# A hybrid encoder trunk on one core: attention maps turned by VectorE in blocks, heads turned by TensorE

## The chip, the cores and the metric

One core of one Trainium2 chip runs the whole program. The metric is the device time of one execution in microseconds (us); lower is better. TensorE does matrix products and transposes, VectorE, ScalarE and GpSimd do the elementwise work, and SyncE issues the transfers.

## The reference

Two requests of 256 tokens (512 columns together) pass two layers of width 1024. All is float32.

```python
for l in range(DEPTH):                                    # DEPTH = 2
    h = rmsnorm(x, g_mix[l])
    u_a, v_a, q, k, v_b, g_a, g_b = split(h @ w_in[l])    # each 1024 wide
    y_a = spatial_gating(u_a, v_a, ...)
    y_b = diff_attention(q, k, v_b, ...)                  # 8 heads, two maps each
    m = sigmoid(g_a) * (y_a @ w_br[l, 0]) + sigmoid(g_b) * (y_b @ w_br[l, 1])
    x = x + m @ w_out[l]
    x = x + conv_gated_mlp(rmsnorm(x, g_ffn[l]), ...)     # 2816 wide, conv of width 3
# diff_attention, for each head and block of 128 queries:
    logits = q @ k.T * scale + bias          # two maps of 256 keys
    p = softmax(logits)
    out = (p[0] - lam * p[1]) @ v            # 128 wide
    out = rmsnorm(out, sub_g) * (1 - lam_init)
```

## The kernel before

Each weight is cut into a high and a low float32r part, and each product of weights is three TensorE passes (high by high, high by low, low by high) of 128 rows and 512 columns. ScalarE writes the high part `w_hi` (lines 555 and 556), VectorE a small piece of the low part `w_lo` (line 986) and GpSimd the rest of it (line 494). A weight slot holds 256 columns of a matrix, and its two halves are two TensorE stretches of 24 passes each.

The attention of a layer has 32 units: a unit is one head, one request and one block of 128 queries, with both of its maps. The order of all engines is written out by hand. The outer loop `r` goes over four pairs of heads, the inner one `i` over the eight units of a pair; the unit's number in the layer is `a = 8 * r + i`. The text calls one step `(r, i)` a window. In a window TensorE runs one half of a slot of the input projection for the next pair (`feature_half` or `token_half`; in the last pair the columns of `u_a`), and behind it `values(a - 2)`, the product of a turned map with the values, then `turn`, which transposes the map of the unit before, and then `logits` of the unit two further on. So the projection is the bulk of the window, and attention's small products stand behind it.

VectorE's window begins, where `i` is even, with the low part of a weight (`split`). It goes on with `softmax_out(i)` (reciprocal, ratio of the two maps and their difference, `attn`), in some windows `head_scale` (which frees the `HEAD` bank for the next head's values) or `head_lo`, then `softmax_in(i + 1)` (bias and maximum). After that come pieces of the head's transpose (`head_move`: VectorE's transpose turns blocks of 32 by 32, so a head of 128 by 512 needs 16 instructions), the low parts of q and k (`qk_lo`) and the evacuation of the projection (`evac_round`, which waits for the window's TensorE half). ScalarE has, in order: the squares of a head and its norm, `w_hi`, the high parts of q and k, the copy of the turned map out of the `TRANS` bank (`turned`, line 654), and the exponentials of the next unit. The queues are in order on each engine, so what stands behind a waiting instruction waits too.

Waits that matter in TensorE's window: `values` needs the turned map (`attn_t_ok`) and, for the first unit of a head (`i` of 2 and 6, since `values` runs two windows late), `head_o_ok` from `head_scale`; the projection needs its weights and a free bank. Slots have two buffers, as have logits, maps and turned maps.

Of the kernel before, what the change touches and what calls it, by code (L numbers as in the profile page):

```python
# [108 lines left out]
def encoder_kernel(nc, x_prompt, x_sample, rel_bias, g_mix, w_in, sgu_g, sgu_w, sgu_b, lam_qk, sub_g,  # L109
# [47 lines left out]
    head_f = sb("head_f", 119, [P, HEADS - 1, N])  # L157
# [17 lines left out]
    head_sq = sb("head_sq", 191, [P, N])  # L175
# [77 lines left out]
    trans_done, attn_t_ok, pv_done = sem("trans_done"), sem("attn_t_ok"), sem("pv_done")  # L253
    head_sq_ok, head_ln_ok, head_rms_ok = sem("head_sq_ok"), sem("head_ln_ok"), sem("head_rms_ok")
    head_wt_ok, head_o_ok, head_t = sem("head_wt_ok"), sem("head_o_ok"), sem("head_t")
    head_moved = sem("head_moved")
# [60 lines left out]

    def moved_n(l, h):

        return l * 4 * (HEADS - 1) + 4 * (h + 1)  # L320
# [218 lines left out]
    def _(sc):  # L539
# [65 lines left out]
        for l in range(DEPTH):  # L605
# [42 lines left out]
            def turned(r, i):  # L648

                a, j, (_h, _r, qt) = 8 * r + i, i // 2, units(i)  # L650
                sc.wait_ge(trans_done, l * UNITS + a + 1)
                if a >= 4:
                    sc.wait_ge(pv_done, l * UNITS + a - 3)
                nc.scalar.activation(attn_t[j % 2][:, :, qt * P:(qt + 1) * P],
                                     bank[TRANS][:, 0:2 * P].rearrange("p (k q) -> p k q", k=2), ACT.Copy)\
                  .then_inc(attn_t_ok, 1)

            def head_square(a):
                h, t = a // 4, a % 4
                sc.wait_ge(pv_done, l * UNITS + a + 1)  # L660
                if a:
                    sc.wait_ge(head_sq_ok, l * UNITS + a)
                nc.scalar.activation(head_sq[:, t * P:(t + 1) * P], bank[HEAD][:, t * P:(t + 1) * P], ACT.Square,
                                     scale=map_inv[:, h % 2, t, 0:1], accum_out=head_ssq[:, t:t + 1]).then_inc(head_sq_ok, 1)
# [10 lines left out]
            def head_hi(h):  # L675
                if h < HEADS - 1:
                    sc.wait_ge(head_moved, moved_n(l, h))
                    turned_head = head_f[:, h, :]
                else:
                    sc.wait_ge(head_t, l + 1)  # L680
                    turned_head = bank[TRANS][:, :]
                nc.scalar.activation(yb_hi[:, h, :], turned_head, ACT.Copy, scale=par[:, C_SUBS:C_SUBS + 1])\
                  .then_inc(yb_hi_ok, 1)
# [54 lines left out]
            for r in range(PAIRS):  # L738
                for i in range(8):
# [9 lines left out]
                    attention_window(r, i)  # L749
                    if r + 1 < PAIRS and i in (4, 5):  # L750
# [27 lines left out]
            turned(PAIRS - 1, 6)  # L778
            head_square(UNITS - 2)
            turned(PAIRS - 1, 7)  # L780
# [116 lines left out]
    def _(ve):  # L897
# [77 lines left out]
        for l in range(DEPTH):  # L975
# [24 lines left out]
            def evac_round(p, place_n, half):  # L1000
# [16 lines left out]
                if n == 3:  # L1017
                    if p == 0 and half == 0:
                        ve.wait_ge(rms_col_ok, l + 1)
                    if p == 2 and half == 0:  # L1020
                        ve.wait_ge(spilled, l * 16 + 16)
                    if p == 3 and half == 0:
                        ve.wait_ge(pv_done, l * UNITS + 16)
# [21 lines left out]
            def softmax_out(r, i):  # L1045
# [9 lines left out]
                if a >= 2:  # L1055
                    ve.wait_ge(trans_done, l * UNITS + a - 1)
                nc.vector.scalar_tensor_tensor(attn[i % 2][:, :], logit[i % 2][:, 1, :], map_ratio[i % 2][:, :],
                                               logit[i % 2][:, 0, :], ALU.mult, ALU.add).then_inc(attn_ok, 1)

            def head_scale(h):  # L1060
# [4 lines left out]
                if h:  # L1065
                    ve.wait_ge(head_moved, moved_n(l, h - 1))
# [4 lines left out]
            def head_move(h, c):  # L1071

                if c == 0:
                    ve.wait_ge(head_o_ok, l * HEADS + h + 1)
                    if h == HEADS - 2:
                        ve.wait_ge(qk_done, l * UNITS + UNITS)
                for a in range(4):
                    src = head_o[32 * a:32 * a + 32, :].rearrange("q (t c d) -> q t c d", t=4, c=4)[:, :, c, :]
                    dst = head_f[32 * c:32 * c + 32, h, :].rearrange("d (t a q) -> d t a q", t=4, a=4)[:, :, a, :]
                    last = nc.vector.transpose(dst, src)  # L1080
                last.then_inc(head_moved, 1)

            def head_lo(h):
                ve.wait_ge(yb_hi_ok, l * HEADS + h + 1)
                turned_head = head_f[:, h, :] if h < HEADS - 1 else bank[TRANS][:, :]
                nc.vector.scalar_tensor_tensor(yb_lo[:, h, :], turned_head, par[:, C_SUBS:C_SUBS + 1],
# [20 lines left out]
            for r in range(PAIRS):  # L1107
                if r == 0:
                    softmax_in(0, 0)
                for i in range(8):  # L1110
                    if i % 2 == 0:
                        split(4 * (r + 1) + i // 2 + 1)
                    softmax_out(r, i)
# [4 lines left out]
                    if r and i == 3:  # L1118
                        head_lo(2 * r - 2)
                    if r and i == 7:  # L1120
# [11 lines left out]
                    if r + 1 == PAIRS and i == 7:  # L1132
                        for c in range(2):
                            head_move(HEADS - 2, c)
# [614 lines left out]
```

## Time and profile before

| what | before |
|---|---|
| median of 3 runs | 1709.09 us (1708.75 to 1709.99) |
| the profiled execution | 1709.8 us, its span 1708.0 us |
| busy share of TensorE, VectorE, ScalarE, GpSimd | 100%, 55%, 44%, 39% |
| granted TensorE clock, mean | 0.999 |

The span is what the profiler records from the first to the last instruction; the time of the execution lies 1.8 us above it. Busy shares are means over the whole span; the attention stages lie at 57 to 267 us and 900 to 1110 us.

### The profile page before, as it was taken

How to read it: one execution, taken by the hardware profiler on the slowest of the kernel's cores; microseconds unless marked ns; L12 is line 12 of the kernel's file. 1: busy time of each engine (PE TensorE's matmuls, PEld its weight loads, DVE VectorE, ACT ScalarE, POOL GpSimd, SP SyncE). 2: the span in 40 equal slices, each digit the busy share in tenths (PEclk: the TensorE clock that was granted, in tenths of full speed). 3: DMA queues.
4: the chain of work that ended last, by engine and by line, in shares of the span. 5: the costliest groups of instructions: out<-in, count | busy, mean ns of one | idle time of the engine just before them, and what ended most of it. 6: DMA issues, size and time to landing. Idle time of an engine off the chain costs nothing.

```text
span 1708.0 us, 22288 instructions
## 1 busy us (share of the span) xinstructions
PE 1699.7 (100%) x7907; PEld 1419.2 (83%) x7907; DVE 945.8 (55%) x1544; ACT 747.7 (44%) x1352; POOL 662.8 (39%) x806
## 2 busy tenths in 40 slices
PE   9999999999999999999999999999999999999998
PEld 7888888888888888888888888888888888888886
DVE  4678876433337766631146888755433476666112
ACT  4676654222345444432256666432223444444222
POOL 3444333333344444434344344333333444444222
PEclk9999999999999999999999999999999999999999
DMA  7422222323232222222353222322242232322222
GB/s 248 135 75 74 87 86 99 99 79 143 98 99 98 98 98 96 92 95 92 108 182 99 75 74 75 124 75 98 74 147 99 96 101 98 98 98 98 87 92 80
DMA packets 146150, 173.93 MB, mean 102 GB/s; under 512 B 2928, under 2 KB 129570, under 8 KB 145570
## 3 DMA queue, kind: packets, MB, share of 16 engines
q1 hardware_dynamic: 145954, 172.96, 30.5%
q8 instruction: 39, 0.64, 0.2%
q14 instruction: 29, 0.24, 0.0%
q10 hardware_dynamic: 128, 0.09, 0.0%
HBM read 166.73 MB, written 6.31 MB: 101 GB/s over the span
## 4 chain that ended last, share of the span: by engine, by line
PE 99%; DVE 0%; ACT 0%; issue 0%; POOL 0%; POOLq 0%; ACTq 0%
PE bank L1448 25%; PE bank L1447 25%; PE bank L1449 25%; PE bank L1482 3%; PE bank L1483 3%; PE bank L1484 3%; PE bank L1719 2%; PE bank L1717 2%; PE bank L1718 2%; PE bank L1505 2%; PE bank L1532 2%; PE bank L1607 1%; PE bank L1516 1%; PE bank L1384 1%; PE bank L1428 1%; PE bank L1637 0%
## 5 line engine op out<-in xcount | busy, mean ns | idle before, releaser
L494 POOL TENSOR_TENSOR w_lo<-raw,w_hi 128x256 fp32r<-128x256 f32 x776 | 627.6, 841 | 1010.0 <-ACT w_hi L556 1010.0
L1447 PE MATMUL bank<-xg_hi,w_hi 128*128 128x512 f32 x1344 | 525.9, 391 | 0.0
L1448 PE MATMUL bank<-xg_lo,w_hi 128*128 128x512 f32 x1344 | 523.4, 389 | 0.0
L1449 PE MATMUL bank<-xg_hi,w_lo 128*128 128x512 f32 x1344 | 523.1, 389 | 0.0
L1449 PEld LDWEIGHTS bank<-xg_hi,w_lo 128*128 128x128 f32 x1344 | 252.3, 188 | 52.7
L1447 PEld LDWEIGHTS bank<-xg_hi,w_hi 128*128 128x128 f32 x1344 | 252.5, 188 | 52.3 <-issue 1.0
L1448 PEld LDWEIGHTS bank<-xg_lo,w_hi 128*128 128x128 f32 x1344 | 252.5, 188 | 51.7 <-issue 1.0
L986 DVE TENSOR_TENSOR w_lo<-raw,w_hi 128x768 fp32r<-128x768 f32 (+2 forms) x146 | 124.9, 856 | 209.9 <-ACT w_hi L555 209.7
L556 ACT ACTIVATE w_hi<-raw 128x1280 fp32r<-128x1280 f32 (+2 forms) x147 | 194.0, 1319 | 0.0
L555 ACT ACTIVATE w_hi<-raw 128x768 fp32r<-128x768 f32 (+2 forms) x147 | 110.4, 751 | 175.1 <-PE bank L1449 90.5
L816 ACT ACTIVATE conv<-up,conv_par 128x512 f32<-128x512 f32 x88 | 71.8, 816 | 129.2 <-DVE up L1248 129.2
L1248 DVE TENSOR_TENSOR up<-bank,rms 128x512 f32<-128x512 f32 x88 | 60.7, 690 | 99.8 <-PE bank L1449 80.6
L1254 DVE SCALAR_TENSOR_TENSOR conv<-up,conv_par,conv 128x510 f32<-128x510 f32 x88 | 77.9, 885 | 47.3 <-ACT conv L816 47.1
L644 ACT ACTIVATE logit<-logit,neg_max 128x256 f32<-128x256 f32 x128 | 64.1, 502 | 89.6 <-DVE neg_max L1042 89.2
L1482 PE MATMUL bank<-w_hi,xg_hi 128*128 128x512 f32 x224 | 87.6, 391 | 0.0
L1483 PE MATMUL bank<-w_hi,xg_lo 128*128 128x512 f32 x224 | 87.5, 390 | 0.0
L1484 PE MATMUL bank<-w_lo,xg_hi 128*128 128x512 f32 x224 | 87.2, 389 | 0.0
L1257 DVE SCALAR_TENSOR_TENSOR conv<-up,conv_par,conv 128x510 f32<-128x510 f32 x88 | 73.8, 839 | 3.1
L1080 DVE STREAM_TRANSPOSE head_f<-head_o 32x128 f32<-32x128 f32 x224 | 67.7, 302 | 3.6
L768 ACT ACTIVATE gate<-gate 128x512 f32<-128x512 f32 x32 | 20.0, 631 | 111.7 <-DVE gate L1207 57.9
L1717 PE MATMUL bank<-w_hi,g_hi 128*128 128x512 f32 x176 | 68.7, 390 | 0.0
L1719 PE MATMUL bank<-w_lo,g_hi 128*128 128x512 f32 x176 | 68.5, 389 | 0.0
(187 smaller groups left out, 2580.1 us busy)
## 6 DMA issues: line engine op xcount, KB each, us to landing
raw<-in_w_in SPq DMA_DIRECT2D x55, 1024.0 KB, 5.1
raw<-in_w_up SPq DMA_DIRECT2D x44, 1024.0 KB, 5.0
raw<-in_w_br SPq DMA_DIRECT2D x16, 1024.0 KB, 5.0
raw<-in_w_down SPq DMA_DIRECT2D x12, 1024.0 KB, 5.0
raw<-in_w_out SPq DMA_DIRECT2D x8, 1024.0 KB, 4.9
raw<-in_w_down SPq DMA_DIRECT2D x8, 896.0 KB, 4.6
x_spill<-x_res SPq DMA_DIRECT2D x2, 2048.0 KB, 7.5
x_res<-x_spill SPq DMA_DIRECT2D x2, 2048.0 KB, 9.5
```

What stands on the lines that cost most here:

```text
L494: last = nc.gpsimd.tensor_tensor(w_lo[p_][:, k, :], raw[p_][:, k, :], f32(w_hi[p_][:, k, :]), ALU.subtract)
L555: nc.scalar.activation(w_hi[s % 2][:, 0:kd(s), :], raw[s % 2][:, 0:kd(s), :], ACT.Copy).then_inc(hi_split, 1)
L556: nc.scalar.activation(w_hi[s % 2][:, kd(s):n, :], raw[s % 2][:, kd(s):n, :], ACT.Copy).then_inc(hi_split, 1)
L986: nc.vector.tensor_tensor(w_lo[p_][:, 0:kd(s), :], raw[p_][:, 0:kd(s), :], f32(w_hi[p_][:, 0:kd(s), :]), ALU.subtract).then_inc(lo_vector, 1)
L1447: nc.tensor.matmul(out, w_hi[w][:, k, cols], x_hi[:, a, :], start=first and k == 0, stop=False)
L1448: nc.tensor.matmul(out, w_hi[w][:, k, cols], x_lo[:, a, :], start=False, stop=False)
L1449: mm = nc.tensor.matmul(out, w_lo[w][:, k, cols], x_hi[:, a, :], start=False, stop=last and k == kt - 1)
L1482: nc.tensor.matmul(bank[t][:, :], xg_hi[:, a, cols], wide_hi[:, k, :], start=first, stop=False)
L1483: nc.tensor.matmul(bank[t][:, :], xg_lo[:, a, cols], wide_hi[:, k, :], start=False, stop=False)
L1484: mm = nc.tensor.matmul(bank[t][:, :], xg_hi[:, a, cols], wide_lo[:, k, :], start=False, stop=last)
L1717: nc.tensor.matmul(out[:, :], g_hi[:, k0 + k, cols], wide_hi[:, k, :], start=c + k == 0, stop=False)
L1719: mm = nc.tensor.matmul(out[:, :], g_hi[:, k0 + k, cols], wide_lo[:, k, :], start=False, stop=last)
```

## The change

The map of a unit is no longer transposed by TensorE. VectorE keeps the maps of two units in one tile (`attn[pair % 2]`, 128 by 2 by 256) and turns both in blocks of 32 by 32 straight into `attn_t` (`turn_maps`). This takes 16 instructions for two units, in two parts of eight: part 0 after `softmax_in` of the odd window, part 1 at the head of the next even window, ahead of its `softmax_out`. Seven of eight heads of a layer, which VectorE turned before, are turned by TensorE as the eighth was (`turn_head`, four transposes, behind `logits` in the windows of `i` 7 and 3), and `head_hi` and `head_lo` read them out of the `TRANS` bank. ScalarE no longer copies turned maps, and evacuates the projected values (two instructions of 128 by 512 in each of the windows 6 and 7) for pairs 1 to 3 with `values_out`; VectorE keeps those of pair 0.

```diff
-    attn = [sb(f"attn{i}", 183 + i, [P, SEQ]) for i in range(2)]
+    attn = [sb(f"attn{i}", kb, [P, 2, SEQ]) for i, kb in enumerate((183, 191))]
...
-            def turned(r, i):
...
+            def values_out(p, half):
+                sc.wait_ge(proj_done, proj_n(l, S_R + 4 * p + 3, half))
+                if p == 2 and half == 0:
+                    sc.wait_ge(spilled, l * 16 + 16)
+                if p == 3 and half == 0:
+                    sc.wait_ge(pv_done, l * UNITS + 16)
+                for t in (2 * half, 2 * half + 1):
+                    dst = va[:, p - 1:p + 1, t, :] if p % 2 else v_tok[p // 2][:, :, t, :]
+                    nc.scalar.activation(dst, bank[t][:, :].rearrange("p (two c) -> p two c", two=2), ACT.Copy,
+                                         scale=rms_col[:, t:t + 1]).then_inc(evacuated, 1)
...
             def attention_window(r, i):
-                if r and i == 2:
+                if r and i == 0:
                     head_hi(2 * r - 2)
-                if r and i == 6:
+                if r and i == 4:
                     head_hi(2 * r - 1)
-                if r and i < 2:
-                    turned(r - 1, 6 + i)
-                if i >= 2:
-                    turned(r, i - 2)
...
                     attention_window(r, i)
+                    if r + 1 < PAIRS and i >= 6:
+                        values_out(r + 1, i - 6)
...
-                if a >= 2:
-                    ve.wait_ge(trans_done, l * UNITS + a - 1)
-                nc.vector.scalar_tensor_tensor(attn[i % 2][:, :], logit[i % 2][:, 1, :], map_ratio[i % 2][:, :],
+                nc.vector.scalar_tensor_tensor(attn[(i // 2) % 2][:, i % 2, :], logit[i % 2][:, 1, :], map_ratio[i % 2][:, :],
...
-            def head_move(h, c):
...
+            def turn_maps(pair, part):
+                if part == 0:
+                    ve.wait_ge(attn_ok, l * UNITS + 2 * pair + 2)
+                    if pair >= 2:
+                        ve.wait_ge(pv_done, l * UNITS + 2 * pair - 2)
+                for c in (2 * part, 2 * part + 1):
+                    for a in range(4):
+                        src = attn[pair % 2][32 * a:32 * a + 32, :, :].rearrange("q u (t c k) -> q u t c k", t=2, c=4)[:, :, :, c, :]
+                        dst = attn_t[pair % 2][32 * c:32 * c + 32, :, :].rearrange("k t (u a q) -> k u t a q", u=2, a=4)[:, :, :, a, :]
+                        last = nc.vector.transpose(dst, src)
+                last.then_inc(attn_t_ok, 1)
...
                     if i % 2 == 0:
                         split(4 * (r + 1) + i // 2 + 1)
+                    if i % 2 == 0 and r + i:
+                        turn_maps(4 * r + i // 2 - 1, 1)
                     softmax_out(r, i)
...
-                    if r and 2 <= i <= 5:
-                        head_move(2 * r - 1, i - 2)
-                    if r and i < 2:
-                        head_move(2 * r - 2, 2 + i)
-                    if r + 1 < PAIRS and i >= 6:
-                        head_move(2 * r, i - 6)
...
+                    if i % 2:
+                        turn_maps(4 * r + i // 2, 0)
...
             def values(a):
-                pe.wait_ge(attn_t_ok, l * UNITS + a + 1)
+                pe.wait_ge(attn_t_ok, l * UNITS + 2 * (a // 2) + 2)
...
                     if a >= 2:
                         values(a - 2)
-                    if a:
-                        turn((a - 1) // 8, (a - 1) % 8)
                     if i + 2 < 8:
                         logits(r, i + 2)
                     elif r + 1 < PAIRS:
                         logits(r + 1, i - 6)
+                    if i == 3 and r:
+                        turn_head(2 * r - 1)
+                    if i == 7:
+                        turn_head(2 * r)
```

## Rows read from the trace of the kernel before

**Rows 1.** The page, busy us (share of the span) and instructions of each engine.
```profile
PE 1699.7 (100%) x7907; PEld 1419.2 (83%) x7907; DVE 945.8 (55%) x1544; ACT 747.7 (44%) x1352; POOL 662.8 (39%) x806
```

**Rows 2.** The page, chain that ended last, by engine.
```profile
PE 99%; DVE 0%; ACT 0%; issue 0%; POOL 0%; POOLq 0%; ACTq 0%
```

**Rows 3.** Windows by head pair, layer 0: length, PE, PEld, DVE, ACT, POOL busy, clock.
```profile
57.56:109.10 51.54, 51.54 (x261) 43.84 (x260) 37.81 (x73) 34.47 (x87) 23.16 (x29) 1.00 0.31 102
109.10:162.00 52.90, 52.90 (x274) 45.21 (x273) 44.48 (x98) 36.52 (x96) 20.75 (x28) 1.00 0.25 80
...
214.82:267.20 52.38, 52.38 (x269) 44.71 (x268) 38.36 (x90) 26.59 (x82) 18.42 (x26) 1.00 0.30 101
```

**Rows 4.** TensorE in order of time, around one window: start, us, engine, line.
```profile
201.61 0.60 PE L1532 MATMUL bank<-v_tok,attn_t 128*128 128x128 f32 x4
202.05 0.38 PE L1516 MATMUL bank<-ident,attn 128*128 128x128 f32 x2
202.19 0.36 PE L1505 MATMUL bank<-k_hi,q_st 128*128 128x256 f32 x1
...
202.75 0.40 PE L1482 MATMUL bank<-w_hi,xg_hi 128*128 128x512 f32 x1
...
208.22 0.61 PE L1532 MATMUL bank<-v_tok,attn_t 128*128 128x128 f32 x4
```

**Rows 5.** TensorE's weight loads in order of time, the same window.
```profile
201.94 0.25 PEld L1516 LDWEIGHTS bank<-ident,attn 128*128 128x128 f32 x2
202.16 0.19 PEld L1505 LDWEIGHTS bank<-k_hi,q_st 128*128 128x128 f32 x1
```

**Rows 6.** The chain in order of time: eight transposes of the gating weights.
```profile
40.50 0.87 PE bank L1574 x8
```

**Rows 7.** VectorE's groups in 109.1 to 162 us: busy, mean ns, idle before, releasers.
```profile
L1080 DVE STREAM_TRANSPOSE head_f<-head_o 32x128 f32<-32x128 f32 x32 | 9.7, 302 | 0.5
...
L996 DVE TENSOR_TENSOR q_st<-qk_f,q_st 64x512 fp32r<-64x512 f32 x4 | 3.6, 909 | 0.1
L1016 DVE TENSOR_TENSOR qk_f<-bank,rms 128x512 f32<-128x512 f32 x4 | 2.8, 691 | 2.3 <-PE bank L1449 2.2
...
L986 DVE TENSOR_TENSOR w_lo<-raw,w_hi 128x256 fp32r<-128x256 f32 x4 | 1.7, 419 | 3.6 <-ACT w_hi L555 3.6
...
L1026 DVE TENSOR_SCALAR v_tok<-bank,rms_col 128x512 f32<-128x512 f32 x2 | 1.4, 747 | 0.0
L1026 DVE TENSOR_SCALAR va<-bank,rms_col 128x512 f32<-128x512 f32 x2 | 1.4, 747 | 1.7 <-PE bank L1484 1.7
```

**Rows 8.** VectorE in order of time: window (2, 6), then (3, 6), then eight transposes.
```profile
203.94 0.42 DVE L986 TENSOR_TENSOR w_lo<-raw,w_hi 128x256 fp32r<-128x256 f32 x1 [2.53 <-ACT w_hi L555]
204.28 0.16 DVE L1050 RECIPROCAL map_inv<-exp_sum 128x2 f32<-128x2 f32 x1
...
205.13 0.16 DVE L1063 TENSOR_TENSOR map_inv<-map_inv,head_rms 128x4 f32<-128x4 f32 x1
...
205.93 0.68 DVE L1038 SCALAR_TENSOR_TENSOR logit<-bank,bias_t 128x512 f32<-128x512 f32 x1
...
207.25 1.24 DVE L1080 STREAM_TRANSPOSE head_f<-head_o 32x128 f32<-32x128 f32 x4
...
256.90 0.96 DVE L986 TENSOR_TENSOR w_lo<-raw,w_hi 128x768 fp32r<-128x768 f32 x1 [1.55 <-ACT w_hi L555]
...
260.39 0.68 DVE L1038 SCALAR_TENSOR_TENSOR logit<-bank,bias_t 128x512 f32<-128x512 f32 x1
...
264.48 2.52 DVE L1080 STREAM_TRANSPOSE head_f<-head_o 32x128 f32<-32x128 f32 x8
```

**Rows 9.** ScalarE in order of time, before the same window.
```profile
203.50 0.40 ACT L555 ACTIVATE w_hi<-raw 128x256 fp32r<-128x256 f32 x1
```

**Rows 10.** ScalarE's groups over the span: busy, mean ns, idle before.
```profile
L691 ACT ACTIVATE junk<-va 128x256 f32<-128x256 f32 x32 | 13.2, 412 | 0.9
...
L682 ACT ACTIVATE yb_hi<-bank,par 128x512 fp32r<-128x512 f32 x2 | 1.4, 690 | 3.2 <-PE bank L1540 3.2
```

More of the change, by code:

```diff
@@ L675, in head_hi @@
             def head_hi(h):
[L676 to L682, printed above, removed]
+                sc.wait_ge(head_t, l * HEADS + h + 1)
+                nc.scalar.activation(yb_hi[:, h, :], bank[TRANS][:, :], ACT.Copy, scale=par[:, C_SUBS:C_SUBS + 1])\
                   .then_inc(yb_hi_ok, 1)
@@ L1017, in evac_round @@
                 if n == 3:
-                    if p == 0 and half == 0:
+                    if half == 0:
                         ve.wait_ge(rms_col_ok, l + 1)
[L1020 to L1023, printed above, removed]
                     for t in (2 * half, 2 * half + 1):
@@ L1069, in head_scale @@
                                         inv.to_broadcast([P, 4, P]), ALU.mult).then_inc(head_o_ok, 1)
-            def head_move(h, c):
[L1073 to L1081, printed above, removed]
+            def turn_maps(pair, part):
[9 more added lines that the diff above has]
+                last.then_inc(attn_t_ok, 1)
             def head_lo(h):
                 ve.wait_ge(yb_hi_ok, l * HEADS + h + 1)
-                turned_head = head_f[:, h, :] if h < HEADS - 1 else bank[TRANS][:, :]
-                nc.vector.scalar_tensor_tensor(yb_lo[:, h, :], turned_head, par[:, C_SUBS:C_SUBS + 1],
+                nc.vector.scalar_tensor_tensor(yb_lo[:, h, :], bank[TRANS][:, :], par[:, C_SUBS:C_SUBS + 1],
                                                f32(yb_hi[:, h, :]), ALU.mult, ALU.subtract).then_inc(yb_lo_ok, 1)
@@ L1117, in _ @@
                         head_scale(2 * r - 1)
-                    if r and i == 3:
+                    if r and i == 0:
                         head_lo(2 * r - 2)
-                    if r and i == 7:
+                    if r and i == 4:
                         head_lo(2 * r - 1)
@@ L1139, in _ @@
                             qk_lo(r + 1, i - 1)
-                        evac_round(r + 1, i // 2, i % 2)
+                        if r and i == 0:
+                            ve.wait_ge(evacuated, evac_n(l, slot_evac(S_R + 4 * r + 3, 1)))
+                        if i < 4:
+                            evac_round(r + 1, i // 2, i % 2)
                     else:
                         s, half = S_U + i // 2, i % 2
+                        if i == 0:
+                            ve.wait_ge(evacuated, evac_n(l, slot_evac(S_U - 1, 1)))
                         ve.wait_ge(proj_done, proj_n(l, s, half))
@@ L1148, in _ @@
                         nc.vector.tensor_reduce(va_rms[:, :], va_sq[:, :, :], AX.X, ALU.add).then_inc(va_sum_ok, 1)
-            for c in range(2, 4):
-                head_move(HEADS - 2, c)
+            turn_maps(UNITS // 2 - 1, 1)
             head_lo(HEADS - 2)
@@ L1508, in logits @@
                 mm.then_inc(qk_done, 1)
-            def turn(r, i):
-                a = 8 * r + i
-                pe.wait_ge(attn_ok, l * UNITS + a + 1)
-                if a:
-                    pe.wait_ge(attn_t_ok, l * UNITS + a)
-                for kt in range(2):
-                    mm = nc.tensor.transpose(bank[TRANS][:, kt * P:(kt + 1) * P], attn[i % 2][:, kt * P:(kt + 1) * P],
-                                             ident[:, :])
-                mm.then_inc(trans_done, 1)
             def values(a):
@@ L1535, in values, with turn_head @@
                 mm.then_inc(pv_done, 1)
-            def turn_last_head():
-                pe.wait_ge(head_o_ok, l * HEADS + HEADS)
+            def turn_head(h):
+                pe.wait_ge(head_o_ok, l * HEADS + h + 1)
+                if h:
+                    pe.wait_ge(yb_lo_ok, l * HEADS + h)
                 for t in range(4):
@@ L1629, in _ @@
                         else:
-                            turn_last_head()
+                            turn_head(HEADS - 1)
                         bank_free(s, half)
```

26 lines of the change are left out of this document (4 added, 22 removed).

## The prediction

> **What bounds the kernel now.** I read the page's busy table and the chain first, then the attention windows by stretch, then each engine's order of time inside one window. TensorE is busy for 1699.7 of 1708.0 us, and the chain is 99% TensorE [rows 1, 2]; the granted clock is full in every attention stretch [rows 3]. So a TensorE instruction taken away shortens the span at once, and work on VectorE costs nothing only while VectorE is ready before TensorE asks. VectorE's 55% is a mean: for the second head pair it is busy 44.48 of 52.90 us, 84%, before anything is added [rows 3]. Inside a window (call V the moment at which TensorE reaches `values`), the period is 208.22 - 201.61 = 6.61 us, of which 208.22 - 202.75 = 5.47 us are the projection and 1.14 us the small products [rows 4].
>
> **TensorE: removed and added.** By starts of matmuls a pair of map transposes takes 202.19 - 202.05 = 0.14 us [rows 4]; by starts of weight loads, which is what these short instructions queue for, 202.16 - 201.94 = 0.22 us [rows 5]. Eight transposes in a row take 0.87 us, 0.11 each [rows 6], which speaks for 0.22; the lower bound is 0.14. 64 units save 64 x 0.22 = 14.1 us (9.0 at the bound). Fourteen heads come back with four transposes each: 56 x 0.11 = 6.1 us. Net -7.9 us, and -2.9 at the bound. A window then takes 6.39 us, the windows 3 and 7 with a head's transposes 6.83; a full pair of heads 52.9 - 8 x 0.22 + 2 x 0.44 = 52.0 us.
>
> **VectorE: the sum.** Its transposes follow each other at 2.52 / 8 = 0.315 us [rows 8]. Before, each of 14 heads takes 16: 224 instructions, 70.6 us. After, each of 32 pairs of units takes 16: 512 instructions, 161.3 us. The tile they write has one more level of stride than before; the page has no such instruction, so from below I take the 302 ns of the plain form [rows 7], which is hardly less, and from above a third more, the ratio of 909 to 691 ns between two elementwise passes over 512 columns [rows 7]: 0.40 us. I take 0.315, since each row is the same 32 by 128 elements. Away from VectorE go 24 evacuations of projected values at 0.75 us [rows 7], 18 us; `head_lo` only changes its source. 161.3 - 70.6 - 18 makes +73 us on VectorE, nearly all of it inside 420 us of attention.
>
> Per head pair: in the second stretch VectorE's true waits are 2.2, 1.7 and 3.6 us, 7.5 together [rows 7], so its order of work takes 52.9 - 7.5 = 45.4 us. It loses 32 transposes (10.1) and four evacuations (3.0) and gains 64 transposes (20.2): 52.5 us, against 52.0 for TensorE. With no wait at all it no longer fits. The first pair comes to 50.8 against 50.4 us (37.8 busy and 0.8 of gaps, less 8 transposes and four evacuations, and 56 transposes more), the last to 49.3 against 51.1 (38.4 and 0.8, 32 less and 64 more) [rows 3].
>
> The Trainium skill (VectorE: DVE Perf Modes, "The three transpose paths") gives 390 ns for TensorE and 311 ns for VectorE on 128 by 128 in bf16, and its "Rules for kernel authors" send a 128 by 128 transpose to TensorE where PSUM will do. By that figure VectorE's 128 map blocks would cost 128 x 0.311 = 40 us, an estimate from that page, and it would have 81 us to spare against the change's sum. The trace has 302 ns for an instruction that covers only 32 partitions [rows 7], so four of them for a block, and its rows decide.
>
> **What then waits.** The turned map and `head_scale` now stand behind eight transposes (8 x 0.315 = 2.53 us) at the head of each even window, and TensorE's `values`, and all behind it, waits for them. Window (2, 6) shows the timing: V of window 5 is 201.61; ScalarE writes `w_hi` from 203.50, VectorE starts `split` at 203.94, V + 2.33 [rows 4, 8, 9]. `softmax_out` runs from 204.28 to 205.13 (0.85) and `head_scale` to 205.93 (0.80) [rows 8]. With part 1 between, `head_o_ok` comes at V + 2.33 + 0.34 + 2.53 + 0.85 + 0.80 = V + 6.85; TensorE's next V is at V + 6.39. That is a stall of 0.45 us where there was none, even if VectorE is never late. In window (3, 6) the low part is larger: from 256.90 to 260.39 are 3.49 us, now 6.02 [rows 8]; V of window 5 is there 201.61 + 8 x 6.61 = 254.46, so `head_o_ok` comes at V + 2.44 + 6.02 = V + 8.46, a stall of 2.1 us.
>
> VectorE's windows, summed from these terms (split 0.34, part 2.53, `softmax_out` 0.85 to 1.3 beside GpSimd, `softmax_in` 1.4 from 205.93 on, `qk_lo` 1.4 to 2.0 around two times the 0.91 us of its row, evacuation 0.61, `head_lo` 0.66): i 0 to 7 take 6.5, 6.9, 8.5, 6.8, 7.9, 4.8, 5.9 and 4.9 us. TensorE's 6.39 or 6.83 lies below that from 1 to 4, so lag piles up there. Walking the second pair from V of the last window of the first pair as zero:
> ScalarE now has `values_out` behind it (two at 0.69, the row of a PSUM read of that size, 0.61 apart [rows 10]) and in every other pair four squares of `va` with their reads, 0.5 apiece, before `w_hi`: VectorE begins window 0 at 4.2 (2.1 in the third pair) instead of 1.4. `values` of window 0 comes at 7.1 (stall 0.3). Window 1 ends on VectorE at 17.6, V of 1 is 13.5. In window 2 `head_o_ok` is at 17.6 + 4.5 = 22.1, TensorE at 19.9: stall 2.2. Window 4: the turned map at 35.8, TensorE at 35.3: 0.5. Window 6: VectorE begins at 45.6, `head_o_ok` at 50.2, TensorE at 48.6: 1.6. The pair ends at 56.6, against 52.9 before: +3.7 us. The third pair by the same walk, with its earlier start, stalls 0.4, 0.5 and 1.5: +1.5. The fourth stalls 0.3, 0.8 and 2.1, less what it saves: +1.9. The first starts without a lead, since in layer 0 its second window already runs late (part 0 puts VectorE's window 2 at V - 0.3): stalls of 2.6, 1.3 and 0.9, +3.5; in layer 1 0.5, 1.2 and 0.9, +1.3. Layer 0: 10.6, layer 1: 8.4, together +19 us with TensorE's saving already in it.
>
> ScalarE loses 64 copies and gets 24 evacuations, a little less in all; it has 16 us free in each stretch [rows 3], so it costs only through the order told above. GpSimd's low parts have some 3 us to spare after `w_hi`, so they hide. The weight transfers hang on GpSimd and are issued that much later, also hidden.
>
> From the profiled execution: 1709.8 + 19 = 1728.8 us; it lies 0.7 above the median, so 1728 for the runs shown.
>
> **Rivals.**
> *VectorE keeps up, TensorE's instructions decide.* Then only the 72 fewer transposes count: 1709.1 - 7.9 = 1701 us (1706 at the bound), faster. For it: TensorE bounds now, and waits of VectorE are 8 us in a pair of heads. Against it: the sum of 52.5 in 52.0, and the 6.85 against 6.39. It decides if VectorE's extra 2.53 us in windows 2 and 6 shrinks below about 2.1. Chance 0.11.
> *Only the order hurts.* VectorE is never behind, the stalls are the fixed ones: 0.45 in window 6 of three pairs, 2.1 in the last, 0.1 in three windows 2, some 3.8 us a layer. 7.6 - 7.9: 1709 us, no change. It holds if VectorE's idle time is enough to soak up the lag, against the sum. Chance 0.09.
> *VectorE saturated, as walked.* 1728 us. Chance 0.68.
> *The new output pattern is slow.* At 0.40 us, 512 x 0.085 = 43 us more, of which seven eighths lie where VectorE already paces: 1728 + 37 = 1765 us. Against it: element counts are the same, only the strides differ. Chance 0.07.
> *The stalls slow the clock.* A gap here is at most 2.6 us, and the records show full clock in all stretches [rows 3]; a fall in the granted clock to half within a stall would double the 0.23 us passes behind it. Nothing in the trace bears it out: 0.05, at around 1745 us.
>
> **The numbers.** A change within 0.2% (3.4 us) can't be told from none. Slower: the last three, 0.80; same: 0.09; faster: 0.11. The range leaves out the fast rival and the slow pattern: from 1709, the fixed stalls alone, to 1746; the likeliest case by itself, with 1 us either way in each pair of heads and VectorE's terms within 2%, 1718 to 1740.
>
> **What would show it.** The chain of waits would name VectorE's transposes and `head_scale` ahead of TensorE's `values` products, 15 to 40 times with 0.3 to 2.6 us each, some 27 us in sum; the stretches would be 53 to 57 us, VectorE above 90% busy in the first three; transposes on VectorE at 302 ns and 512 in number; TensorE's `values` followed at once by `logits`, 0.22 us sooner. It is wrong if the stretches come out near 52 us with no idle time on TensorE, if the transposes have another duration, or if the wait is on ScalarE's evacuation of values.

## The result, and the profile after

The changed kernel takes 1777.49 us (median of 5 runs, 1776.53 to 1779.67) against 1709.09 (1708.75 to 1709.99): ratio 1.0401, 95% interval 1.039 to 1.0412. That is 68 us slower, where 19 was predicted. The profiled execution has a span of 1774.7 us against 1708.0, so 66.7 us are to be found in the trace. From the page of the changed kernel: busy us of each engine; the chain of work that ended last, followed back from the last instruction, by engine; and two groups of instructions (busy, mean ns of one, idle before, releaser).

```profile
PE 1717.9 (97%) x7835; PEld 1426.5 (80%) x7835; DVE 1029.1 (58%) x1808; ACT 741.4 (42%) x1312; POOL 659.1 (37%) x806
...
PE 79%; DVE 15%; ACT 3%; issue 3%; POOL 0%; ACTq 0%; POOLq 0%
...
L1061 DVE STREAM_TRANSPOSE attn_t<-attn 32x128 f32<-32x128 f32 x512 | 154.7, 302 | 7.2
...
L1501 PE MATMUL bank<-v_tok,attn_t 128*128 128x128 f32 x256 | 43.6, 296 | 48.8 <-DVE head_o L1047 42.0
```

Two things differ from [rows 1, 2]. TensorE was idle for 8.3 us in all and is now for 56.8, of which 48.8 stand in front of the `values` products: 21 waits, 14 of them for `head_o` (42.0 us) and the other seven for `attn_t` (6.8 us). And TensorE's busy time went *up* by 18.2 us with 72 instructions fewer. Instructions that got fewer and yet busier are running slower, and the windows say so. Stretches of the attention part of layer 0: length, PE, PEld, DVE, ACT, POOL busy, the granted clock, DMA share, GB/s.

```profile
57.00:110.00 53.00, 46.86 (x217) 38.99 (x216) 45.70 (x105) 28.62 (x64) 21.53 (x29) 0.94 0.24 80
110.00:167.00 57.00, 52.27 (x254) 44.03 (x255) 48.06 (x116) 37.39 (x98) 15.72 (x22) 0.94 0.23 74
167.00:222.00 55.00, 49.52 (x235) 41.25 (x234) 48.03 (x113) 28.39 (x69) 20.48 (x28) 0.94 0.20 67
222.00:280.00 58.00, 51.30 (x242) 42.65 (x241) 45.27 (x115) 28.25 (x81) 18.50 (x26) 0.94 0.20 65
```

The clock of 1.00 of [rows 3] is 0.94 in each. TensorE in order of time around the first wait shows where it falls (start, us of one, idle before in brackets):

```profile
79.02 1.22 PE L1501 MATMUL bank<-v_tok,attn_t 128*128 128x128 f32 x4 [3.55 <-DVE attn_t L1061]
79.89 0.56 PE L1484 MATMUL bank<-k_hi,q_st 128*128 128x256 f32 x1
...
81.32 0.63 PE L1427 MATMUL bank<-xg_lo,w_hi 128*128 128x512 f32 x1
81.74 0.63 PE L1428 MATMUL bank<-xg_hi,w_lo 128*128 128x512 f32 x1
...
84.66 0.40 PE L1426 MATMUL bank<-xg_hi,w_hi 128*128 128x512 f32 x1
84.90 0.40 PE L1427 MATMUL bank<-xg_lo,w_hi 128*128 128x512 f32 x1
...
88.09 0.60 PE L1501 MATMUL bank<-v_tok,attn_t 128*128 128x128 f32 x4
88.45 0.36 PE L1484 MATMUL bank<-k_hi,q_st 128*128 128x256 f32 x1
...
94.47 0.60 PE L1501 MATMUL bank<-v_tok,attn_t 128*128 128x128 f32 x4
```

```profile
76.00:80.00 4.00, 0.98 (x5) 0.98 (x5) 3.77 (x13) 0.84 (x2) 3.04 (x5) 0.72 0.00 0
80.00:84.00 4.00, 4.00 (x14) 3.32 (x13) 3.82 (x8) 2.01 (x7) 0.00 (x0) 0.50 0.78 262
84.00:88.00 4.00, 4.00 (x18) 3.29 (x17) 3.84 (x11) 3.05 (x8) 0.00 (x0) 0.93 0.00 0
```

The second fence has the stretches of the same place, columns as above. After a wait of 3.55 us passes of 512 columns start 0.42 us apart (81.32 to 81.74) instead of 0.24 (84.66 to 84.90), at a granted clock of 0.50, the lower level, 1.2 GHz; from 84.66 on it is the full one. This window lasts 88.09 - 79.02 = 9.07 us, where the next, undisturbed one lasts 94.47 - 88.09 = 6.38. So this wait costs 3.55 us and then 2.7 us more. The other waits of layer 0, read in the same way, cost 1.6 to 1.7 us behind 1.83, 2.25, 2.84, 3.23 and 3.58 us of waiting and 2.3 behind 4.41; the wait of 2.62 us cost 0.1 behind it, and those of 0.29 us 0.1. Layer 1 has waits of the same length with another price: one of 2.25 us at 1049.27 us costs 1.7 behind it, at a granted clock of 0.67 to 0.79, and one of 2.25 us at 1110.46 costs 0.1, at a clock of 1.00; its wait of 1.83 us costs 0.1, where that of layer 0 cost 1.7. So the length of a wait doesn't fix its price. The Trainium skill (TensorE: Matmul & The Clock Gate, "Part 1: The HAM clock gate") has a clock that falls to half when the array has been idle; the trace agrees behind 12 of the 21 waits, all of 1.83 us or more, and shows no such price behind the other nine, the longest of 2.62 us (granted clock 1.00 in and behind it).

**The sum.** Waits +48.8 us; transposes -7.9 as worked out; that leaves 66.7 - 48.8 + 7.9 = 25.8 us that are neither. By the lengths of the windows, the slower stretches behind the 21 waits are 13.6 us in layer 0 and 10.2 in layer 1, and a window that ends in a wait is 0.16 us longer than its like (6.55 for 6.39), 3.4 us in all. That makes 27, so the sum closes within 1.4 us, and 23 of it stand behind the 12 waits with the lower clock.

### The profile page after: what moved, and what is told of

It reads as the page before. It is cut to its first block, busy times and chain, and to the rows that moved or that the text cites. A ratio compares the mean times of both kernels' runs of the same rounds, so it can differ in the third digit from the quotient of the medians.

```text
span 1774.7 us, 22236 instructions
## 1 busy us (share of the span) xinstructions
PE 1717.9 (97%) x7835; PEld 1426.5 (80%) x7835; DVE 1029.1 (58%) x1808; ACT 741.4 (42%) x1312; POOL 659.1 (37%) x806
## 4 chain that ended last, share of the span: by engine, by line
PE 79%; DVE 15%; ACT 3%; issue 3%; POOL 0%; ACTq 0%; POOLq 0%
PE bank L1426 21%; PE bank L1427 21%; PE bank L1428 21%; DVE attn_t L1061 5%; PE bank L1689 2%; PE bank L1690 2%; PE bank L1691 2%; DVE attn L1037 1%; DVE logit L1020 1%; PE bank L1463 1%; PE bank L1462 1%; DVE neg_max L1024 1%; PE bank L1461 1%; DVE map_ratio L1034 1%; DVE q_st L982 1%
## 5 line engine op out<-in xcount | busy, mean ns | idle before, releaser
L1426 PE MATMUL bank<-xg_hi,w_hi 128*128 128x512 f32 x1344 | 531.6, 396 | 0.0
L972 DVE TENSOR_TENSOR w_lo<-raw,w_hi 128x768 fp32r<-128x768 f32 (+2 forms) x146 | 126.6, 867 | 212.2 <-ACT w_hi L549 211.9
L1061 DVE STREAM_TRANSPOSE attn_t<-attn 32x128 f32<-32x128 f32 x512 | 154.7, 302 | 7.2
L1501 PE MATMUL bank<-v_tok,attn_t 128*128 128x128 f32 x256 | 43.6, 296 | 48.8 <-DVE head_o L1047 42.0
L1501 PEld LDWEIGHTS bank<-v_tok,attn_t 128*128 128x128 f32 x256 | 39.1, 202 | 60.6 <-issue 47.5
```

The costliest lines, as they stand in the source:

```text
L972: nc.vector.tensor_tensor(w_lo[p_][:, 0:kd(s), :], raw[p_][:, 0:kd(s), :], f32(w_hi[p_][:, 0:kd(s), :]), ALU.subtract).then_inc(lo_vector, 1)
L1426: nc.tensor.matmul(out, w_hi[w][:, k, cols], x_hi[:, a, :], start=first and k == 0, stop=False)
```

## Why head_o comes late: the moved work meets GpSimd

VectorE in order of time in window (0, 6), the case worked out ahead as V + 6.85, then GpSimd in the same window:

```profile
103.82 0.42 DVE L972 TENSOR_TENSOR w_lo<-raw,w_hi 128x256 fp32r<-128x256 f32 x1 [1.40 <-ACT w_hi L549]
104.28 2.53 DVE L1061 STREAM_TRANSPOSE attn_t<-attn 32x128 f32<-32x128 f32 x8
106.84 0.17 DVE L1032 RECIPROCAL map_inv<-exp_sum 128x2 f32<-128x2 f32 x1
107.04 0.57 DVE L1034 SCALAR_TENSOR_TENSOR map_ratio<-map_inv,par,exp_sum 128x1 f32<-128x1 f32 x1
107.65 0.91 DVE L1037 SCALAR_TENSOR_TENSOR attn<-logit,map_ratio 128x256 f32<-128x256 f32 x1
108.48 0.68 DVE L1043 TENSOR_TENSOR map_inv<-map_inv,head_rms 128x4 f32<-128x4 f32 x1
109.19 0.69 DVE L1047 TENSOR_TENSOR head_o<-bank,map_inv 128x512 f32<-128x512 f32 x1
109.80 0.68 DVE L1020 SCALAR_TENSOR_TENSOR logit<-bank,bias_t 128x512 f32<-128x512 f32 x1
```

```profile
105.46 5.05 POOL L488 TENSOR_TENSOR w_lo<-raw,w_hi 128x256 fp32r<-128x256 f32 x7 [9.19 <-ACT w_hi L550]
```

V is 100.86 here. The instruction behind `head_o` starts at 109.80, V + 8.94. Term by term against the 6.85: the split begins at V + 2.96 (2.33), the split takes 0.46 (0.34), the transposes 2.56 (2.53), `softmax_out` 1.64 (0.85), `head_scale` 1.32 (0.80). Before, `softmax_out` and `head_scale` ran directly behind the split and were nearly done when GpSimd's low part began; put back by 2.5 us, they lie in the middle of its 5.05 us. The product of a map of 256 columns takes 0.91 instead of 0.48 us (the first line below, from the kernel before) and the 4-column product of `head_scale` 0.68 instead of 0.16 [rows 8]. The two together take 2.96 us instead of 1.65. In C (the change, as it is called below) this happens to 12 of the 14 heads that TensorE waits for: their small product takes 0.68 us with GpSimd at work throughout, and the two steps together 2.63 to 2.98. The transposes (one input) and the two instructions that read PSUM (`head_o` 0.69, `logit` 0.68) keep their times.

```profile
204.73 0.48 DVE L1057 SCALAR_TENSOR_TENSOR attn<-logit,map_ratio 128x256 f32<-128x256 f32 x1
...
205.57 4.91 POOL L494 TENSOR_TENSOR w_lo<-raw,w_hi 128x256 fp32r<-128x256 f32 x7 [9.00 <-ACT w_hi L556]
```

The Trainium skill (SBUF — State Buffer, "SBUF: two separate sides") has a port pair that VectorE and GpSimd hold by an exclusive lock, on VectorE's side for instructions with two inputs in SBUF against a GpSimd instruction that reads SBUF. The instructions just listed agree with it. Over the traces of all versions the 4-column product takes 0.15 to 0.17 us wherever GpSimd's records leave it free, and 0.65 to 0.70 where they cover it, with five exceptions: in number 12 below it takes 0.15 twice (at 254.89 and 282.13 us) and 0.54 once, in number 11 twice 0.41. So GpSimd at work doesn't slow it in every place, which no run here explains.

The price stood in the trace of the kernel before, in the one window of each layer where `softmax_out` and `head_scale` already run beside GpSimd. It is window (3, 6), whose whole length the prediction used and whose parts it didn't look at:

```profile
258.23 0.91 DVE L1057 SCALAR_TENSOR_TENSOR attn<-logit,map_ratio 128x256 f32<-128x256 f32 x1
259.06 0.70 DVE L1063 TENSOR_TENSOR map_inv<-map_inv,head_rms 128x4 f32<-128x4 f32 x1
...
258.12 3.69 POOL L494 TENSOR_TENSOR w_lo<-raw,w_hi 128x256 fp32r<-128x256 f32 x5 [8.88 <-ACT w_hi L556]
```

## The experiments

Times are medians; each ratio is against the kernel before on the same chip. TensorE's waits are those listed in front of the `values` products. The change is named C, and a band is the range of times that an expectation gave.

**1. Part 1 of the turned map behind head_scale, in windows 2 and 6.**

```
 softmax_out(r, i); head_scale(...)
+if i % 4 == 2:
+    turn_maps(4 * r + i // 2 - 1, 1)      # was ahead of softmax_out
```

> Only the order on VectorE is changed: in windows 2 and 6 the second part of the map transposes stands behind head_scale, not ahead of softmax_out. Theory A (place and GpSimd: 14 of the 21 waits of values are for head_o, 42.0 of 48.8 us, because eight transposes stand ahead of softmax_out and head_scale and push both into GpSimd's low part, where they took 2.96 instead of 1.65 us): the two go back to about 1.7 us, values waits for the turned map instead, each wait is 1.2 us shorter, 17 us in all, and with shorter waits the half clock goes in part: 1745 to 1760 us. Theory B (VectorE is simply full, the order is nothing): within 5 us of 1777. Both: 512 transposes at 302 ns.

1759.53 us, ratio 1.0286 (1.0262 to 1.0311), its four runs from 1755.1 to 1763.5: 18 us of the 68 come back. `softmax_out` and `head_scale` are back at 1.77 us in eight of the 14 places and take 2.67 to 3.04 in the six that still have GpSimd beside them. The waits are 39.7 us, 39.5 of them for `attn_t`: windows 2 and 6 need both the turned map and `head_o`, so an exchange of the two mostly changes the name of what is late.

**2. All 16 transposes of a pair in the odd window.**

```
 if i % 2:
     turn_maps(4 * r + i // 2, 0)
+    turn_maps(4 * r + i // 2, 1)
```

> Both parts of the map transposes stand in the odd window, behind softmax_in, and none at the head of an even window. Theory A: head_scale comes 2.5 us sooner after VectorE's even window begins, window 5, which has room, takes the part that stood in window 6, so the waits before windows 6 nearly vanish and those before windows 2 shrink: 1725 to 1745 us, better than scale_first. Theory B (VectorE is full): the same 161 us of transposes are in the queue, 1765 to 1780 us.

1761.94 us, 1.031 (1.0292 to 1.0327), waits 41.7 us, again mostly for `head_o`. It fell between the two expectations, and by its runs (1759.6 to 1765.1) it can't be told from number 1. `softmax_out` and `head_scale` still take 2.86 to 3.08 us in all 14 places: with no transposes ahead of them in the window, VectorE is late enough that GpSimd's low part is under way when it gets there.

**3. TensorE kept busy in front of the head_o waits** (20 transposes of the identity ahead of each of the 14).

```
 if a % 4 == 0 and a:
+    for _ in range(20):
+        nc.tensor.transpose(bank[TRANS][:, 0:P], ident[:, :], ident[:, :])
     pe.wait_ge(head_o_ok, l * HEADS + a // 4)
```

> Twenty transposes of the identity (2.2 us) are added on TensorE ahead of each of the 14 waits for head_o (all of them into a part of a PSUM bank that is free), nothing else. The waits are 2.3 to 4.4 us long, so the added work lies inside them. Theory C (the half clock behind each wait, mean granted clock 0.983 over the span, is a cost of its own, up to 30 us): the granted clock comes back to 1.00 in the stretches behind the waits, and the time falls to 1750 to 1765 us although work was added. Rival (only the waits count, the clock falls into time that is lost anyway): 1775 to 1785 us.

1764.06 us, 1.0324 (1.0306 to 1.0341): 13.4 us *less* than C, with 280 matmuls added and `head_o` no earlier by design. The same wait as above at 109 us, and its stretches (columns as above):

```profile
106.04 2.40 PE L1500 MATMUL bank<-ident 128*128 128x128 f32 x20 [0.25 <-DVE attn_t L1061]
109.10 0.71 PE L1505 MATMUL bank<-v_tok,attn_t 128*128 128x128 f32 x4 [0.66 <-DVE head_o L1047]
```

```profile
57.00:112.00 55.00, 50.54 (x249) 42.13 (x249) 46.65 (x109) 30.33 (x70) 21.55 (x28) 0.97 0.25 80
112.00:167.00 55.00, 52.48 (x269) 43.49 (x267) 47.42 (x116) 36.13 (x94) 15.93 (x23) 1.00 0.22 74
167.00:222.00 55.00, 52.82 (x284) 44.74 (x285) 49.66 (x116) 30.21 (x75) 19.71 (x27) 1.00 0.24 77
```

The clock is 1.00 in the stretches behind the filled waits, and 0.97 in the one that holds the unfilled wait for `attn_t`. The windows behind the filled waits last 6.47 to 6.50 us (the last of each layer 5.9), near the 6.39 of an undisturbed one; in C 11 of the 14 last 7.6 to 8.9. This shows the slow clock as a cost of its own, apart from the idle time. Only 13.4 us come back and not 20, presumably because VectorE is late for a quicker TensorE too; that was not measured.

**4. Half of the map transposes left out** (256 of 512 transposes; TensorE's instructions as in C; the turned tiles are set to zero once in each layer).

```
-for c in (2 * part, 2 * part + 1):
+for c in (2 * part,):
```

> Half of the map transposes is left out (four instead of eight instructions in each part, 256 fewer, so half of the turned maps is zero and the values' products are incomplete); a clearing of the two tiles is added once in each layer (about 1 us on VectorE). All waits, their order and TensorE's instructions stay. If VectorE's time is all that costs, with about 42 of 52 us in a pair of heads it is ready in time: 1701 to 1706 us, TensorE's 7.9 us saving shown whole. If another part of the change costs (the values evacuated by ScalarE, the heads' transposes in the TRANS bank, a chain of waits), 1715 us or more.

1724.81 us, 1.0095 (1.0078 to 1.0112). VectorE has 81 us less to do, more than the 73 that the change adds, so by its sum it would keep up; the clock is full (0.999), and still TensorE waits 18.8 us. That is the second case of the expectation, 1715 us or more, by a cause that it didn't list: `softmax_out` and `head_scale` take 2.83 to 2.87 us in 12 of the 14 places (2.59 in the other two). So VectorE's sum is only part of the story. Its waits for `head_o` (releaser; us, times, longest):

```profile
PE bank L1505 <- DVE head_o L1047: 17.4, 14, 2.3
```

**5. The same with part 1 behind head_scale in windows 2 and 6** (edits 4 and 1 together).

> As half_turned (half of the map transposes left out, half of the turned maps zero), and the second part stands behind head_scale in windows 2 and 6. In half_turned 20 us of waits were left, nearly all for head_o, with VectorE far from full. Theory A (place and GpSimd): softmax_out and head_scale run before GpSimd's low part and take 1.65 instead of 2.83 us, head_o comes some 2.5 us sooner, no wait is left: 1700 to 1705 us. Theory B (something else, for instance ScalarE's later w_hi, delays VectorE's even windows): waits of 10 us and more stay, 1712 us or more.

1710.75 us, 1.0004 (0.9995 to 1.0014). All 14 waits for `head_o` are gone; 5.4 us in four waits for `attn_t` are left. The distance to number 4 is 14 us for a place in the order alone, and the two steps are at 1.77 us in 12 of the 14 places. The time is still above theory A's band of 1700 to 1705: the waits that are left, the longest of 3.01 us with 1.4 us behind it, were to be none. TensorE's window lasts 178.04 - 171.65 = 6.39 us in its trace, the figure worked out ahead:

```profile
171.65 0.60 PE L1507 MATMUL bank<-v_tok,attn_t 128*128 128x128 f32 x4
...
178.04 0.60 PE L1507 MATMUL bank<-v_tok,attn_t 128*128 128x128 f32 x4
```

**6. C with the values evacuated by VectorE again.**

```
-if r + 1 < PAIRS and i >= 6:
-    values_out(r + 1, i - 6)            # ScalarE
-if i < 4:
-    evac_round(r + 1, i // 2, i % 2)
+evac_round(r + 1, i // 2, i % 2)        # VectorE, all rounds
```

> The change with one part undone: the projected values of pairs 1 to 3 are evacuated by VectorE again. If VectorE's time sets the pace, 24 instructions of 0.75 us come back on a full engine: 1785 to 1800 us. Rival (ScalarE's evacuations delay w_hi and with it VectorE's window 0 by 2 to 4 us, which is a cost of the change): 1765 to 1777 us.

1765.44 us, 1.0321 (1.0304 to 1.0339): 12 us less than C, though the evacuations add 18 us of work to the engine that is late. TensorE's waits fall from 48.8 to 42.8 us. C's trace shows where: ScalarE at the end of the first head pair, then VectorE, behind it.

```profile
116.69 1.27 ACT L681 ACTIVATE va<-bank,rms_col 128x512 f32<-128x512 f32 x2 [0.93 <-PE bank L1463]
117.85 0.42 ACT L670 ACTIVATE junk<-va 128x256 f32<-128x256 f32 x1
...
120.29 0.41 ACT L549 ACTIVATE w_hi<-raw 128x256 fp32r<-128x256 f32 x1
```

```profile
120.73 0.42 DVE L972 TENSOR_TENSOR w_lo<-raw,w_hi 128x256 fp32r<-128x256 f32 x1 [3.69 <-ACT w_hi L549]
```

`w_hi` stands behind two evacuations and four squares of `va` on ScalarE, and VectorE is idle for 3.69 us until it comes. Over the whole span VectorE waits 211.9 us for `w_hi` in C and 188.3 here.

**7. The kernel before with that evacuation on ScalarE, and nothing else.**

> The kernel before with one part of the change alone: the projected values of pairs 1 to 3 are evacuated by ScalarE. TensorE's instructions are those of before and nobody waits: 1709 us, within 1 us. If ScalarE's evacuations delay w_hi past what TensorE can bear: 1712 us or more.

1708.8 us, 0.9997 (0.9988 to 1.0007). Alone it costs nothing, although VectorE waits for `w_hi` longer, 237.4 us over the span where the kernel before has 209.7: TensorE doesn't come to wait for it. So the same edit costs 0 or 12 us, by who waits behind VectorE in turn.

**8. Three of four pairs of units on VectorE, the third by TensorE and ScalarE**, with part 1 behind `head_scale` in window 2.

> A mixed version with the whole computation: of the four pairs of units in a pair of heads, VectorE turns three, and the third (units 4 and 5) goes through TensorE and the copy by ScalarE as before; in window 2 the second part stands behind head_scale. VectorE's order is some 47.5 us of 52. TensorE saves 48 x 0.22 = 10.6 us and gets 6.1 us of heads back: 1704.7 us if it never waits. Theory A: 1705 to 1710 us. Theory B (VectorE must be far below full before TensorE stops waiting, since the lag of windows 1 to 4 is what counts): 1715 to 1730 us.

1744.8 us, 1.0208 (1.0191 to 1.0225); waits 27.2 us, the large ones (2.1 to 5.1 us) all for `attn_t` at window 2. That is slower than both expectations had it: the relief stood at window 6, the crowd at window 2.

**9. The first of four pairs by TensorE and ScalarE instead**, both parts of the third in window 5.

```
+if i in (1, 2):
+    turn(r, i - 1)                       # TensorE; ScalarE copies it out
-if i % 2 == 0 and r + i:
+if i in (0, 4) and r + i:
     turn_maps(4 * r + i // 2 - 1, 1)
-if i % 2:
+if i % 2 and i > 1:
     turn_maps(4 * r + i // 2, 0)
+if i == 5:
+    turn_maps(4 * r + 2, 1)
```

> Another mixed version with the whole computation, three of four pairs of units turned by VectorE as in three_of_four, but the pair that TensorE and ScalarE turn is the first (units 0 and 1, whose parts stood in windows 1 and 2), and both parts of the third pair stand in window 5. No part of the transposes is left in windows 2 and 6. If the lag of windows 0 to 2 is what three_of_four lost 35 us to (its waits were for the turned map of pair 0, 12 of 14 us in layer 0), it goes: 1704 to 1710 us, with 0.3 to 0.5 us at window 0 of some head pairs left. If VectorE's total of some 47.5 of 52 us is too much in any order: 1720 us or more.

1729.65 us, 1.0121 (1.0106 to 1.0137), the second case of the expectation, though number 11 will show that its reason, too large a total in any order, is not the one: eight waits for `head_o` of 1.04 to 2.64 us are left, and seven small ones of at most 0.47.

**10. Number 9 with the values on VectorE**, as in number 6.

> As first_by_tensor, with the projected values of pairs 1 to 3 evacuated by VectorE again. In values_vector the same step back took 12 us off the change although it loads VectorE. If what counts is that ScalarE writes w_hi in time, this is as fast as first_by_tensor or 1 to 3 us faster, 1703 to 1708 us; if VectorE's sum counts (47.5 + 3 of 52 us), it is 5 us or more slower.

1721.99 us, 1.0076 (1.0062 to 1.0089), 7.7 us less than number 9: the effect of number 6 a second time, and larger than the 1 to 3 us expected; the time stays above both bands. Its waits for `head_o` are eight, 1.05 to 2.34 us, one for each pair of heads, at window 6, behind 16 transposes (5.06 us) in window 5.

**11. Number 10 with head_scale at the head of VectorE's windows 2 and 6**, ahead of the split and of `softmax_out`, so ahead of GpSimd's low part too.

```
+if i == 6: head_scale(2 * r)
+if r and i == 2: head_scale(2 * r - 1)
 if i % 2 == 0: split(4 * (r + 1) + i // 2 + 1)
 ...
 softmax_out(r, i)
-if i == 6: head_scale(2 * r)
-if r and i == 2: head_scale(2 * r - 1)
```

> The kernel that turns the first of four pairs of units by TensorE and ScalarE, the other three by VectorE, with the values evacuated by VectorE (1722 us, eight waits of 1.05 to 2.34 us for head_o), with one edit: head_scale now stands at the very head of VectorE's windows 2 and 6, ahead of the split and of softmax_out. Theory A, the waits that are left are the place of head_scale behind softmax_out beside GpSimd's low part (softmax_out and head_scale took 3.0 us there): the eight waits, 13.3 us, go, and the time is that of TensorE's instructions, 48 pairs of transposes less (10.6 us) and 56 transposes more (6.1 us): 1703 to 1708 us. Rival B, VectorE has no slack left at that place (16 transposes of 5.06 us stand in window 5 ahead of it) and what is moved behind head_scale comes late in its turn: waits for attn_t or on the softmax of 1 us or more in place of those for head_o, 1713 to 1722 us.

1711.23 us, 1.0011 (1.0002 to 1.002). All eight waits for `head_o` are gone, as theory A had it, but the time is 3 us above its band. VectorE, then TensorE, in order of time:

```profile
125.92 0.17 DVE L1059 TENSOR_TENSOR map_inv<-map_inv,head_rms 128x4 f32<-128x4 f32 x1 [0.87 <-ACT head_rms L658]
126.12 0.69 DVE L1063 TENSOR_TENSOR head_o<-bank,map_inv 128x512 f32<-128x512 f32 x1
126.73 0.42 DVE L982 TENSOR_TENSOR w_lo<-raw,w_hi 128x256 fp32r<-128x256 f32 x1
```

```profile
149.61 0.68 PE L1517 MATMUL bank<-v_tok,attn_t 128*128 128x128 f32 x4
156.30 0.68 PE L1517 MATMUL bank<-v_tok,attn_t 128*128 128x128 f32 x4
...
189.91 0.60 PE L1517 MATMUL bank<-v_tok,attn_t 128*128 128x128 f32 x4
190.83 0.60 PE L1540 MATMUL bank<-ident,head_o 128*128 128x128 f32 x4
196.74 0.60 PE L1517 MATMUL bank<-v_tok,attn_t 128*128 128x128 f32 x4
```

The small product takes 0.17 us again. The matmuls show 2.4 us of waits in seven; the window from 149.61 to 156.30 lasts 6.69 us where 6.39 is due, with no wait written at its matmuls. There it is the weight loads that wait (0.48 us at 156.27). Over the kernel those of `values` do so 9 times by the sequencer's issue (4.1 us) and 7 times for `attn_t` (4.7 us), which overlap in part with the 2.4. So what was won on TensorE (48 pairs of transposes less, 10.6 us, and 56 transposes more, 6.1 us) is eaten by many small waits; VectorE is busy for 52.3 of 55 us in the third stretch of layer 0.

**12. All pairs on VectorE, all 16 transposes in the odd window, head_scale first, values on VectorE**: the best order found, for C's whole set of transposes.

> The change with all maps turned by VectorE, but with the values evacuated by VectorE again, all 16 transposes of a pair of units in the odd window, and head_scale at the very head of windows 2 and 6. Theory A, most of the waits are order, not VectorE's sum: of 42.8 us of waits with the values on VectorE under 15 are left, 1712 to 1730 us. Rival B, VectorE's 52.5 us of work per pair of heads against TensorE's 52.0 is the bound whatever the order: waits of 30 us or more stay, with the slowed clock behind them, 1745 to 1765 us.

1752.34 us, 1.0253 (1.0237 to 1.0268). This is theory B's outcome: 35.1 us of waits stay, now 23.0 of them for ScalarE's `head_sq` and 10.3 for `head_o`, and VectorE is busy for 51.6 of 55 us in the third stretch. Behind the two longest waits for `head_sq` (4.34 and 3.87 us) stands VectorE too: ScalarE had itself waited 2.14 us for VectorE's `neg_max` (until 158.03 us in the first case), and its exponentials and a copy of `k_lo` then stand ahead of the square at 160.43. This trace has the same small instruction beside GpSimd's low part and ahead of one:

```profile
135.34 0.65 DVE L1045 TENSOR_TENSOR map_inv<-map_inv,head_rms 128x4 f32<-128x4 f32 x1
...
166.71 0.16 DVE L1045 TENSOR_TENSOR map_inv<-map_inv,head_rms 128x4 f32<-128x4 f32 x1
```

```profile
132.98 5.94 POOL L488 TENSOR_TENSOR w_lo<-raw,w_hi 128x256 fp32r<-128x256 f32 x7 [8.53 <-ACT w_hi L550]
...
167.15 5.28 POOL L488 TENSOR_TENSOR w_lo<-raw,w_hi 128x256 fp32r<-128x256 f32 x7 [12.43 <-ACT w_hi L550]
```

No version beat the kernel before.

## Why the prediction was right or wrong

**Direction right, mechanism right in part.** The chain names VectorE's `attn_t` transposes (5% of the span by themselves) ahead of TensorE's `values`, as forecast. But the likeliest case was a saturated VectorE, above 90% busy in stretches of 53 to 57 us, and C is not that: its first three head pairs in layer 0 last 62.2, 61.7 and 62.6 us, with VectorE busy for 53.1, 53.1 and 51.8 of them, 83 to 86%, and idle for 16.6 us in all before `w_hi`. VectorE's own work came out near its sum (52.5); the rest of the 62 us is engines in fixed orders that wait for each other. VectorE's sum comes near to being the limit only where those waits are taken away: in number 12 a pair still lasts 60.9 us with VectorE busy for 57.3, 94%. With the whole set of transposes 35 to 42 us of waits stay in each order tried (numbers 1, 2 and 12). Numbers 4 and 5 show the order as a cause by itself, worth 14 us even where the sum fits.

**TensorE's terms: right.** A window of 6.39 us is measured in number 5, one with a head's transposes is 196.74 - 189.91 = 6.83 in number 11, and in C `logits` follows 0.36 us after `values` instead of 0.58. Net -7.9 us stands. Two slips changed little: the last pair of heads gets two heads' transposes, not one, which makes it 51.5 us and not 51.1; and beside the page's 40 us the trace's 161.3 are 121 us more, not 81.

**The transposes: right.** 512 of 302 ns, 0.315 us apart (2.53 for eight); the rival of a slow output pattern is out. The start of window 0 at V + 4.2 behind ScalarE's evacuations came at 120.73 with V at 116.50: V + 4.23.

**The waits: mechanism right, size wrong.** This is the term that was mis-sized: "some 27 us in sum", 0.3 to 2.6 us each, measured 48.8 us in 21 waits, 0.28 to 4.41 each. For the second pair the walk gave 0.3, 2.2, 0.5 and 1.6; the trace has 0.29, 4.41, none and 2.25. The step that failed is `head_o_ok` at "V + 2.33 + 0.34 + 2.53 + 0.85 + 0.80": the last two durations were read where these instructions ran *ahead of* GpSimd's low part and used where they run *beside* it. The prediction priced the neighbour for `softmax_out` in the windows' sums (up to 1.3), not in this term, and for `head_scale` nowhere. Measured are 2.63 to 2.98 us in place of 1.65 in 12 of 14 heads, 15 us in sum, of the 22 that the waits lie above the forecast. In window (3, 6), where the prediction used the length of a row that had the neighbour in it, its 2.1 us of stall came out as 1.83. In window (0, 6) another 0.6 us came from `w_hi` (V + 2.96 for 2.33). That GpSimd's low parts "hide" was true of GpSimd and false of what stands beside them. That each of these microseconds reaches TensorE's waits, and what else makes up the 22, is argued and not measured.

**ScalarE's evacuation: right place, not priced apart.** I had it cost "only through the order", and it did: 12 us in C (number 6), 8 in number 9, nothing in the kernel before.

**The slow clock: wrong chance.** I gave 0.05 to stalls that slow the clock, as a rival to the saturated case, because the gaps I had walked were at most 2.6 us. It was no rival but a second part of the same case: some 25 us, put at nothing in the likeliest sum, of which number 3 gives 13 back although it adds 280 matmuls. Had I carried the mechanism with the sum, 1745 us would have been the likeliest time; with the waits sized right as well, -7.9 + 48.8 + 25 makes 1775.

**Not settled.** Why waits of the same length, 2.25 and 1.83 us, cost 1.7 us in one place and 0.1 in another no run here tells. The lag in windows 1 and 2 was not divided between GpSimd and ScalarE. What 56 more transposes cost in the kernel before, by themselves, was not measured; the 0.22 us of a pair and the 0.11 of one rest on the lengths of windows, 6.61, 6.39 and 6.83 us.

## What to carry to other kernels

A duration belongs to a place: before an instruction is moved, look which engine is at work beside the new place, and take its duration from a row with the same neighbour. When TensorE bounds and is given waits of some microseconds, count them once for the idle time and once for the slower passes behind them: about half as much again here in sum, with the single wait at 0.1 or at 1.5 to 2.7 us. And an edit that is free in one kernel (number 7) can cost ten microseconds in another, where somebody waits behind the engine that it delays (number 6): price edits of one change together, in the order that they leave.

## What was unexpected of the hardware

A product over 128x4 elements on VectorE takes 0.16 us alone and mostly 0.65 to 0.70 us beside GpSimd's elementwise pass, with the five exceptions above, and one over 128x256 takes 0.48 and 0.91; 32x128 transposes (0.302 us) and instructions that read PSUM (0.69 us) don't change. TensorE's passes of 512 columns, started 0.23 to 0.24 us apart, are 0.42 us apart, from 80.89 to 84.30, after a wait of 3.55 us (granted clock 0.50), though its records show no gap there; the same wait of 2.25 us is followed by the lower clock once and by the full one another time. And a kernel got 13.4 us faster by 20 useless transposes ahead of each of 14 waits.
